# Cache pages on two DMA queues, GEMM pieces one step earlier in long head rows, and gate memsets behind a weight split

## The chip, the cores and the metric

One Trainium2 chip, one of its cores. The metric is the device time of one launch in microseconds (us), lower is better. The engines are named as in the profile: PE (TensorE, matmul), PEld (its weight loads), DVE (VectorE), ACT (ScalarE), POOL (GpSimd) and SP (SyncE, which only issues DMAs).

## What is computed

The reference is one inference step of a two-layer decoder, run for a prompt group (1 x 1024 tokens) and for a sample group (8 sequences x 4 tokens) that share all weights; `D_MODEL` is 1024.

```python
# layer 0: gated width-3 convolution (512 channels) beside differential attention, 4 heads
attn = diff_attend(q, k, v, causal_mask, lam)                    # prompt: own keys
past_k = cache_k[j, page_table].reshape(nb, -1, DA_HEADS, 128)   # samples: 2048 cached keys each
past_v = cache_v[j, page_table].reshape(nb, -1, DA_HEADS, 128)
attn = diff_attend(q, concat(past_k, k), concat(past_v, v), mask, lam)
h = h + rmsnorm(concat([y_conv, attn]) @ w_out0, g[1]);  h = h + rmsnorm(swiglu(rmsnorm(h, g[2])), g[3])
# layer 1: mLSTM, 4 heads of width 256, gates from two more columns per head, chunkwise scan
h = h + rmsnorm(mlstm(rmsnorm(h, g[0]) @ w_in1) @ w_out1, g[1]);  h = h + rmsnorm(swiglu(...), g[3])
```

The cache of the samples is 8 sequences x 16 pages x 128 tokens, for keys and for values, so 256 pages of 128 x 512 float32 (256 KB). Which page is read is known only from `page_table`.

## The kernel before

All 1056 tokens (1024 + 32) lie along the free dimension. A weight matrix is worked through in **visits**: a visit is one panel of 128 output columns (`VISITS`, its weight tile is 512 KB), and has three **units**, each a third of the tokens (352) in one PSUM bank. A weight tile is loaded by SP into one of two buffers (`load_tile`, L200), split by ACT and DVE into a high and a low float16 part (`split_hi`, L218; `split_lo`, L231), and a unit is 24 matmuls (L248). `panel(..., ring=...)` (plan at L270 to L320) says which PSUM banks a visit's units take in turn; a unit waits until the one before it in its bank has been evacuated by ACT or DVE.

Every engine has its instruction stream written out by hand. Where a chain of dependent steps with waits (attention of a head, the sample attention, an mLSTM chunk) runs beside a GEMM, both are Python generators, and `woven(chunk, fill, between)` interleaves them: after each step of the chunk it takes as many steps of the GEMM as the table `between` says. A GEMM step on PE is half a unit, 12 matmuls; the same table is used on PE, ACT, DVE and, for the samples, SP, so a number that moves in it moves work on all of them.

- **Heads of the prompt attention** (`pe_head`, `act_head`, `dve_head`, table `HEAD_FILL`). A head has 8 rows of 128 queries. A row i of 4 or more has three chunk steps on PE: scores of row i+1 and transposes of the first four probability tiles (L843, L846, L908), transposes of the rest (L908), and probabilities times values (L922). The last one waits for the copies of the transposed tiles out of PSUM by ACT (L973) and DVE (L1064). `dve_mixed` (L1002 to L1004) makes the weights of row i+1, and the first transposes of row i+1 wait for them.
- **Sample attention** (`pe_samples`, table `SAMPLE_FILL`). Two rounds of four sequences. In a round come 32 steps on key pages (two pages in a step are transposed, L1155, and multiplied with the queries, L1143), a softmax, and 32 steps on value pages (L1194). Pages go through a ring of 16 buffers. `load_page` reads the page number into a register (L1088), waits until the buffer's last page is used, and issues the DMA (L1092). All pages are issued by SP, in `sp_samples`, woven with the `load_tile` calls of the GEMM beside it. POOL meanwhile waits for the last page (L2061), to restore `hT` from its spill.
- **Start of layer 1** (`act_gates`, `dve_gate_zeros`, `dve_gates`, `dve_mlstm`). POOL spills `hT` to HBM (L2077); gate rows, masks and states then take its place. `dve_gate_zeros` (L1435 to L1440) waits for the spill and clears them. `dve_gates` is the chain of gate computations, taken step by step between the evacuations of the first head's projections (`dve_qkvo`); ACT takes part in it (`act_gate_logs`, L1422, L1424) before it evacuates its first unit (L1509). The projections of one mLSTM head are 8 visits, 24 units, in banks 6 and 7.

Of the kernel before, what the change touches and what calls it, by code (L numbers as in the profile page):

```python
# [72 lines left out]
def build(nc, x_p, x_s, cache_k, cache_v, state_conv, state_C, state_n, state_m, page_table, norms, w_in0,  # L73
# [3 lines left out]
    with ctx:  # L77
# [229 lines left out]
        for i in range(HEADS):  # L307
            for m in range(8):
                c0 = (m // 2) * D + (m % 2) * P + i * MLD
                panel(w_cols(w_in1[0], slice(c0, c0 + P)), KD, "dve" if m in (2, 3) else "act", ring=(6, 7))  # L310
# [504 lines left out]
        HEAD_FILL = (0,) + (1,) * 5 + (1, 0) * 3 + (1, 1) + (1, 0, 1) * 4  # L815
# [269 lines left out]
        def load_page(sp, f):  # L1085

            cache, b, p = (cache_k, cache_v)[f // 64 % 2], 4 * (f // 128) + f // NPG % 4, f % NPG
            page = sp.value_load(page_ids[0:1, b * NPG + p:b * NPG + p + 1], min_val=0,  # L1088
                                 max_val=cache_k.shape[1] - 1)
            if f >= RING:  # L1090
                sp.wait_ge(page_used, f - RING + 1)
            sp.dma_start(ring[:, f % RING, :], cache[0, ds(page, 1), :, :, :].rearrange("a t h e -> (a t) (h e)")  # L1092
                         ).then_inc(page_loaded[f % RING // 2], 16)

        def sp_samples(sp):
            f = RING
            for _ in range(3):
                yield
            for _ in range(2):
                for _ in range(32):  # L1100
                    for f in range(f, min(f + 2, 256)):
                        load_page(sp, f)
                    f += 1
                    yield
                for _ in range(4):
                    yield
                for _ in range(32):
                    for f in range(f, min(f + 2, 256)):
                        load_page(sp, f)
                    f += 1  # L1110
                    yield
                for _ in range(3):
                    yield
# [328 lines left out]
        def dve_gates(dve, chain):  # L1442

            drained(dve, last_unit(GATES))
# [524 lines left out]
        def _(sp):  # L1969
# [28 lines left out]
            for f in range(RING):  # L1998
                load_page(sp, f)
# [14 lines left out]
        def _(pool):  # L2014
# [35 lines left out]
            pool.sem_inc(const_ready, 1)  # L2050

# [8 lines left out]
            pool.dma_start(v_s[0].rearrange("b t h e -> (b t) h e"), kv_s_nat[:, 1, :, :]).then_inc(rows_saved, 16)  # L2060
            pool.wait_ge(page_used, 2 * NB * NPG)  # L2061
# [108 lines left out]
        def _(dve):  # L2170
# [41 lines left out]
            dve_gate_zeros(dve, chain)  # L2212
# [89 lines left out]
```

## Time and profile before

| | |
|---|---|
| median of 3 runs | 3062.14 us (3059.71 to 3066.23) |
| profiled execution | 3063.34 us, of which the span of the trace is 3061.6 us |
| granted TensorE clock, mean | 0.964 |
| PE, PEld, DVE, ACT, POOL busy | 92%, 61%, 34%, 27%, 7% |
| moved by DMA | 225.5 MB, 74 GB/s over the span |

The stages by the trace, in us from the start of the span: prompt heads to about 370, sample attention to 682, output projection and first FFN to about 1588, mLSTM to about 2240, second FFN and output to the end. A busy share of PE near 100% over a whole stage says only that it is not idle; what matters is each place where it is idle, and what ended that.

### The profile page before, as it was taken

The page shows a single profiled execution, that of the slowest core. Times are in us where ns is not written, and L with a number is a line of the kernel's source. Part 1 is how long each engine was busy: PE and PEld are TensorE (multiplying, and loading weights), DVE is VectorE, ACT ScalarE, POOL GpSimd, SP SyncE. Part 2 cuts the span into 40 slices and gives each one's busy share as a digit, 9 for nine tenths or more (in the row PEclk, how much of TensorE's full clock was granted, in tenths as well). Part 3 has the DMA queues.
Part 4 walks back from the last instruction along what each step waited for, and adds up shares of the span by engine and source line. Part 5 has one row for each costly group of instructions (what it writes and reads, how often), then busy time and mean ns, then how long its engine had stood idle before and what let it go on. Part 6 is the DMA issues. An engine that isn't in the chain of part 4 may idle for free.

```text
span 3061.6 us, 46331 instructions
## 1 busy us (share of the span) xinstructions
PE 2831.3 (92%) x19359; PEld 1863.7 (61%) x19359; DVE 1043.0 (34%) x1743; ACT 831.3 (27%) x1523; POOL 210.4 (7%) x189
## 2 busy tenths in 40 slices
PE   6988898979699999999969999999978999999997
PEld 4665554546466666666635767666645666666665
DVE  4454541412622211222263343344454221122223
ACT  4444431313322212221132333333333222122211
POOL 2000000002200000000120010101131000000010
PEclk8999998999799999999989999999989999999998
DMA  5211177771011211112226232422221111111111
GB/s 185 63 56 37 39 217 234 229 250 49 14 49 49 59 45 42 55 50 57 33 63 65 35 87 34 88 47 66 75 78 42 49 51 57 38 50 55 57 40 57
DMA packets 259018, 225.51 MB, mean 74 GB/s; under 512 B 10308, under 2 KB 217466, under 8 KB 258300
## 3 DMA queue, kind: packets, MB, share of 16 engines
q1 hardware_dynamic: 251196, 183.02, 23.3%
q0 software_dynamic: 7616, 39.53, 3.5%
q8 instruction: 155, 2.54, 0.3%
q14 instruction: 51, 0.42, 0.0%
HBM read 195.70 MB, written 26.81 MB: 73 GB/s over the span
## 4 chain that ended last, share of the span: by engine, by line
PE 83%; DVE 6%; SPq 3%; issue 3%; ACT 2%; DMA 2%; POOL 1%; DVEq 0%; ACTq 0%; POOLq 0%; PEldq 0%
PE ps L248 68%; DVE arena L521 2%; PE ps L1155 2%; PE ps L922 1%; SPq L1088 1%; SPq L1092 1%; PE ps L843 1%; PE ps L1716 1%; PE ps L1707 1%; PE ps L1685 1%; POOL arena L334 1%; PE ps L1660 1%; PE ps L1699 1%; PE ps L1143 1%; DVE arena L444 1%
## 5 line engine op out<-in xcount | busy, mean ns | idle before, releaser
L248 PE MATMUL ps<-u,w_split 128*128 128x352 f16 (+1 forms) x10440 | 1625.9, 316 | 67.4 <-DVE u L470 38.7
L248 PEld LDWEIGHTS ps<-u,w_split 128*128 128x128 f16 (+1 forms) x10440 | 1023.5, 99 | 631.5 <-DVE u L470 44.2
L248 PE MATMUL ps<-arena,w_split 128*128 128x352 f16 x4320 | 651.9, 313 | 0.0
L248 PEld LDWEIGHTS ps<-arena,w_split 128*128 128x128 f16 x4320 | 422.1, 98 | 223.9 <-issue 3.2
L231 DVE SCALAR_TENSOR_TENSOR w_split<-w_raw,w_split 128x1024 f16<-128x1024 f32 (+2 forms) x194 | 269.1, 1387 | 835.8 <-ACT w_split L218 835.7
L218 ACT ACTIVATE w_split<-w_raw 128x1024 f16<-128x1024 f32 (+2 forms) x194 | 211.6, 1090 | 84.4 <-PE ps L248 76.2
L577 ACT ACTIVATE arena<-arena 128x352 f16<-128x352 f32 x132 | 65.6, 497 | 390.1 <-DVE arena L609 390.1
L609 DVE SCALAR_TENSOR_TENSOR arena<-ps,arena 128x352 f32<-128x352 f32 x132 | 69.2, 524 | 287.3 <-PE ps L248 287.3
L571 ACT ACTIVATE arena<-ps 128x352 f32<-128x352 f32 x132 | 60.8, 463 | 329.3 <-PE ps L248 329.3
L1509 ACT ACTIVATE arena<-ps 128x352 f32<-128x352 f32 x72 | 33.2, 463 | 207.7 <-PE ps L248 207.6
L331 POOL COPY arena<-arena 128x1056 f32<-128x1056 f32 x4 | 4.3, 1063 | 1227.5 <-ACT arena L590 1203.3
L334 POOL TENSOR_TENSOR arena<-arena 128x1056 f32<-128x1056 f32 x28 | 68.5, 2447 | 236.1 <-ACT arena L590 175.6
L1155 PE MATMUL ps<-ident,hT 128*128 128x128 f32 x512 | 70.4, 281 | 9.0 <-DMA hT<-in_cache_k 7.2
L1155 PEld LDWEIGHTS ps<-ident,hT 128*128 128x128 f32 x512 | 56.2, 142 | 33.1 <-issue 17.7
L585 ACT ACTIVATE arena<-ps 128x352 f32<-128x352 f32 x48 | 22.2, 463 | 193.3 <-PE ps L248 193.3
L626 DVE SCALAR_TENSOR_TENSOR arena<-ps,arena 128x352 f32<-128x352 f32 x48 | 25.0, 521 | 142.3 <-PE ps L248 142.3
L590 ACT ACTIVATE arena<-arena 128x1056 f32<-128x1056 f32 x16 | 17.3, 1083 | 202.2 <-DVE arena L626 202.2
L603 DVE TENSOR_TENSOR arena<-arena 128x352 f16<-128x352 f32 x132 | 68.4, 518 | 8.8 <-ACT arena L577 8.8
L1281 DVE COPY arena<-ps 128x512 f32<-128x512 f32 x64 | 44.2, 691 | 69.4 <-PE ps L1155 69.0
L405 PE MATMUL ps<-arena,ones 128*128 128x352 f32 x144 | 53.4, 530 | 15.3 <-ACT arena L342 15.1
L995 DVE TENSOR_REDUCE small<-ps 128x1 f32<-128x128 f32 (+7 forms) x64 | 45.5, 752 | 60.0 <-PE ps L846 60.0
L1194 PE MATMUL ps<-hT,arena 128*4 128x128 f32 x1024 | 40.1, 291 | 27.2 <-DMA hT<-in_cache_v 27.2
(337 smaller groups left out, 2020.8 us busy)
## 6 DMA issues: line engine op xcount, KB each, us to landing
w_raw<-in_w_gu SPq DMA_DIRECT2D x88, 512.0 KB, 3.8
hT<-in_cache_k SPq DMA_DIRECT2D x128, 256.0 KB, 3.1
hT<-in_cache_v SPq DMA_DIRECT2D x128, 256.0 KB, 3.1
w_raw<-in_w_in SPq DMA_DIRECT2D x56, 512.0 KB, 6.4
w_raw<-in_w_down SPq DMA_DIRECT2D x32, 704.0 KB, 4.6
h_spill<-hT POOLq DMA_DIRECT2D x2, 4224.0 KB, 13.2
hT<-h_spill POOLq DMA_DIRECT2D x2, 4224.0 KB, 13.7
hT<-in_state_C POOLq DMA_DIRECT2D x32, 256.0 KB, 4.2
```

The source lines that it names most:

```text
L218: act.activation(w_split[:, v % 2, 0, 0:kt * n], w_raw[:, v % 2, 0:kt * n], ACT.Copy, scale=WS).then_inc(w_hi, 1)
L231: dve.scalar_tensor_tensor(w_split[:, v % 2, 1, 0:kt * n], w_raw[:, v % 2, 0:kt * n], WS, w_split[:, v % 2, 0, 0:kt * n], ALU.mult, ALU.su ...
L248: ins = pe.matmul(ps[0:m, bank, 0:GW], w_split[:, v % 2, wp, k * w + col * P:k * w + col * P + m], x[:, xp, k0 + k, cols(g)], start=(k == ...
L334: pool.tensor_tensor(ssq, ssq, sq[k % 2], ALU.add).then_inc(ssq_added, 1)
L405: ins = pe.matmul(ps[:, root_bank(n) + g, 0:GW], ones[:, :], sq[k % 2][:, g * GW:(g + 1) * GW], start=(k == 0), stop=(k == KD - 1))
L521: dve.scalar_tensor_tensor(tmp[k % 4], hT[:, k, :], gains[:, col + k:col + k + 1], rs, ALU.mult, ALU.mult).then_inc(t_ready, 1)
L571: act.activation(gate[:, cols(g)], ps[:, UNITS[n].bank, 0:GW], ACT.Silu, scale=1 / WS).then_inc(evac["act"], 1)
L577: act.activation(hid[:, 0, i, cols(g)], hidf[:, cols(g)], ACT.Copy).then_inc(hid_hi, 1)
L603: dve.tensor_tensor(hid[:, 1, i, cols(g)], hidf[:, cols(g)], hid[:, 0, i, cols(g)], ALU.subtract).then_inc(hid_ready, 1)
L609: dve.scalar_tensor_tensor(hidf[:, cols(g)], ps[:, UNITS[n].bank, 0:GW], 1 / WS, gate[:, cols(g)], ALU.mult, ALU.mult).then_inc(evac["dve" ...
L995: dve.tensor_reduce(neg_mx[:, n % 4:n % 4 + 1], score_cols(i, c)[:, 0:(i + 1) * P], AX.X, ALU.max, negate=True).then_inc(nm_ready, 1)
L1155: ins = pe.transpose(ps[:, 4 + e, h * P:(h + 1) * P], ring[:, f % RING, h * P:(h + 1) * P], ident[:, :])
```

## The change

1. **Pages on two queues.** Pages f with f // 2 odd (2, 3, 6, 7, ...) are issued by POOL, the others by SP. POOL issues its 8 pages of the first 16 after it has built `smask`, and the other 120 after it has stored the keys and values of the prompt and the new rows of the samples, in one loop, ahead of its wait for the last page. SP keeps its steps; in every second one it issues nothing.
2. **`HEAD_FILL`** in rows 4 to 7: the table for a row is (1, 1, 0) in place of (1, 0, 1), so the second GEMM piece of the row runs ahead of the product with the values instead of after it.
3. **Gate memsets.** `dve_gate_zeros` moves from ahead of `dve_mlstm` into the first step of `dve_gates`, behind the split of the second projection tile. The projections of the first mLSTM head use banks 1 to 7 in turn instead of 6 and 7.

```diff
-                panel(w_cols(w_in1[0], slice(c0, c0 + P)), KD, "dve" if m in (2, 3) else "act", ring=(6, 7))
+                panel(w_cols(w_in1[0], slice(c0, c0 + P)), KD, "dve" if m in (2, 3) else "act",
+                      ring=(6, 7) if i else (1, 2, 3, 4, 5, 6, 7))
...
-        HEAD_FILL = (0,) + (1,) * 5 + (1, 0) * 3 + (1, 1) + (1, 0, 1) * 4
+        HEAD_FILL = (0,) + (1,) * 5 + (1, 0) * 3 + (1, 1) + (1, 1, 0) * 4
...
                 for _ in range(32):
-                    for f in range(f, min(f + 2, 256)):
+                    if f // 2 % 2 == 0 and f < 2 * NB * NPG:
                         load_page(sp, f)
-                    f += 1
+                        load_page(sp, f + 1)
+                    f += 2
                     yield
...
         def dve_gates(dve, chain):
 
+            dve_gate_zeros(dve, chain)
+            yield
             drained(dve, last_unit(GATES))
...
             for f in range(RING):
-                load_page(sp, f)
+                if f // 2 % 2 == 0:
+                    load_page(sp, f)
...
             pool.sem_inc(const_ready, 1)
+            pool.wait_ge(ids_loaded, 16)
+            pool.wait_ge(x_spilled, 16)
+            pool.wait_ge(t_ready, KD)
+            for f in range(RING):
+                if f // 2 % 2:
+                    load_page(pool, f)
...
             pool.dma_start(v_s[0].rearrange("b t h e -> (b t) h e"), kv_s_nat[:, 1, :, :]).then_inc(rows_saved, 16)
+            for f in range(RING, 2 * NB * NPG):
+                if f // 2 % 2:
+                    load_page(pool, f)
             pool.wait_ge(page_used, 2 * NB * NPG)
...
             split_lo(dve, QKVO)
-            dve_gate_zeros(dve, chain)
             dve_mlstm(dve, chain)
```

How the instructions stand in the two programs, at the three places of which the prediction speaks. (Line numbers of the changed program run a little ahead: L1093 is L1092 before, L923 is L922, L1438 is L1435.)

POOL, behind the last stores of the prompt heads. Before:

```order
L2059 DMA out<-kv_s_nat 32x512 [waits k_ev,v_ev]
L2060 DMA out<-kv_s_nat 32x512
L2062 DMA hT<-h_spill 128x8448 [waits page_used]
L2064 DMA out<-arena 2x512 [waits conv_ev]
L2065 DMA out<-arena 16x512
```

POOL at the same place in the changed program:

```order
L2071 DMA out<-kv_s_nat 32x512 [waits k_ev,v_ev]
L2072 DMA out<-kv_s_nat 32x512
L1089 TENSOR_LOAD page_ids
L1089 ISA x2
L1093 ISA [waits page_used]
L1093 DMA hT<-in_cache_k 128x512
```

The last four rows repeat 120 times (for keys and values), and SP has as many of them fewer. The eight earlier ones stand ahead of the stores of the heads.

PE, row 5 of a head. Before:

```order
L908 MATMUL ps<-ident,arena 128x128 [waits pt_ev_act,w_comb]
L908 MATMUL ps<-ident,arena 128x128
L922 MATMUL ps<-arena 128x128 [waits v_ev,pv_ev,pt_ev_dve,pt_ev_act]
L922 MATMUL ps<-arena 128x128 x5
L248 MATMUL ps<-u,w_split 128x352 x12
L843 MATMUL ps<-arena 128x512 [waits p_ready]
```

PE in the changed program, the same row 5:

```order
L909 MATMUL ps<-ident,arena 128x128 [waits pt_ev_act,w_comb]
L909 MATMUL ps<-ident,arena 128x128
L248 MATMUL ps<-u,w_split 128x352 x12
L923 MATMUL ps<-arena 128x128 [waits v_ev,pv_ev,pt_ev_dve,pt_ev_act]
L923 MATMUL ps<-arena 128x128 x5
L844 MATMUL ps<-arena 128x512 [waits p_ready]
```

The piece of 12 GEMM matmuls now stands between the transposes and the product that waits for their copies; the scores of the next row follow the product directly.

DVE at the start of layer 1, before:

```order
L231 SCALAR_TENSOR_TENSOR w_split<-w_raw,w_split 128x1024 [waits w_hi]
L1435 MEMSET hT 4x1056 [waits spilled]
L1436 MEMSET hT 4x8 [waits dve_c]
L1437 MEMSET hT 4x8
L1438 MEMSET m_prev 4x1
L1439 MEMSET acol 128x108
L1440 MEMSET hT 128x576
L231 SCALAR_TENSOR_TENSOR w_split<-w_raw,w_split 128x1024 [waits w_hi]
L1445 SCALAR_TENSOR_TENSOR arena<-arena 4x1056 [waits evac_act]
```

DVE at the start of layer 1 in the changed program:

```order
L231 SCALAR_TENSOR_TENSOR w_split<-w_raw,w_split 128x1024 [waits w_hi] x2
L1438 MEMSET hT 4x1056 [waits spilled]
L1439 MEMSET hT 4x8 [waits dve_c]
L1440 MEMSET hT 4x8
L1441 MEMSET m_prev 4x1
L1442 MEMSET acol 128x108
L1443 MEMSET hT 128x576
L1450 SCALAR_TENSOR_TENSOR arena<-arena 4x1056 [waits evac_act]
```

The second split now stands ahead of the wait for the spill; the gate chain still stands behind it.

## Rows read from the trace of the kernel before

**Rows 1.** The page: chain that ended last, shares of the span by line.

```profile
PE ps L248 68%; DVE arena L521 2%; PE ps L1155 2%; PE ps L922 1%; SPq L1088 1%; SPq L1092 1%; PE ps L843 1%; PE ps L1716 1%; PE ps L1707 1%; PE ps L1685 1%; POOL arena L334 1%; PE ps L1660 1%; PE ps L1699 1%; PE ps L1143 1%; DVE arena L444 1%
```

**Rows 2.** Windows: length, PE, PEld, DVE, ACT, POOL busy (instructions), clock, DMA share, GB/s.

```profile
64.00:81.00 17.00, 17.00 (x116) 11.01 (x115) 2.27 (x3) 2.03 (x4) 0.55 (x2) 1.00 0.81 240
622.00:667.00 45.00, 30.15 (x440) 16.54 (x432) 7.77 (x15) 1.55 (x2) 0.00 (x0) 0.89 0.81 246
```

**Rows 3.** Timeline of SP's queue: start, length of the series, line, what, how many.

```profile
63.62 17.68 SPq L1092 DMA_DIRECT2D hT<-in_cache_k  x16
...
445.22 1.06 SPq L200 DMA_DIRECT2D w_raw<-in_w_in  x2
452.60 34.89 SPq L1092 DMA_DIRECT2D hT<-in_cache_v  x26
```

**Rows 4.** The page: DMA issues, count, KB each, median us from issue to landing.

```profile
hT<-in_cache_v SPq DMA_DIRECT2D x128, 256.0 KB, 3.1
...
hT<-in_state_C POOLq DMA_DIRECT2D x32, 256.0 KB, 4.2
```

**Rows 5.** Timeline of PE, sample attention: start, us, [idle before <- what ended it].

```profile
452.00 0.62 PE L1194 MATMUL ps<-hT,arena 128*4 128x128 f32 x16
457.32 3.68 PE L248 MATMUL ps<-u,w_split 128*128 128x352 f16 x12 [4.71 <-DVE arena L807]
...
517.89 0.62 PE L1194 MATMUL ps<-hT,arena 128*4 128x128 f32 x16
528.64 1.04 PE L1155 MATMUL ps<-ident,hT 128*128 128x128 f32 x8
...
591.21 0.90 PE L1166 MATMUL ps<-arena 128*32 128x32 f32 x32
611.22 0.62 PE L1194 MATMUL ps<-hT,arena 128*4 128x128 f32 x16
617.13 1.49 PE L1194 MATMUL ps<-hT,arena 128*4 128x128 f32 x48
671.02 0.62 PE L1194 MATMUL ps<-hT,arena 128*4 128x128 f32 x16
```

**Rows 6.** Chain in order of time, first key pass: start, us, what.

```profile
387.53 1.90 PE ps L248 x12
...
402.02 1.90 PE ps L248 x12
```

**Rows 7.** Timeline of POOL: DMAs it issues.

```profile
293.24 0.90 POOL L2055 DMA_DIRECT2D out<-arena  x1 [2.63 <-DVE arena L1041]
...
1673.80 2.92 POOL L2091 DMA_DIRECT2D hT<-in_state_C  x4 [27.91 <-ACT hT L1431]
```

**Rows 8.** Waits of PE in the prompt heads (us in total, times, longest).

```profile
PE ps L922 <- issue: 22.5, 16, 4.5
```

**Rows 9.** Timeline of PE and DVE, heads 1 and 3.

```profile
195.28 1.96 PE L922 MATMUL ps<-arena 128*128 128x128 f32 x12 [3.39 <-issue]
197.03 3.28 PE L248 MATMUL ps<-u,w_split 128*128 128x352 f16 x12
218.89 1.09 PE L870 MATMUL ps<-ident,arena 128*128 128x128 f32 x8 [0.80 <-ACT arena L725]
337.81 2.90 PE L922 MATMUL ps<-arena 128*128 128x128 f32 x12 [4.54 <-issue]
339.13 1.28 DVE L756 SCALAR_TENSOR_TENSOR arena<-arena,gains 128x1024 f32<-128x1024 f32 x1
```

**Rows 10.** Timeline of all engines at the start of layer 1.

```profile
1594.57 10.13 PE L248 MATMUL ps<-u,w_split 128*36 128x352 f16 x66 [0.77 <-DVE u L470]
1599.90 1.04 ACT L218 ACTIVATE w_split<-w_raw 128x1024 f16<-128x1024 f32 x1
1605.04 0.94 DVE L1435 MEMSET hT<- 4x1056 f32 x1 [8.15 <-DMA h_spill<-hT]
1613.23 32.06 PE L248 MATMUL ps<-u,w_split 128*128 128x352 f16 x204 [8.54 <-ACT arena L1509]
```

More of the change, by code:

```diff
@@ L1083, in build, with load_page @@
         SAMPLE_FILL = (1, 1, 0) + ROUND_FILL * 2
-        def load_page(sp, f):
+        def load_page(eng, f):
             cache, b, p = (cache_k, cache_v)[f // 64 % 2], 4 * (f // 128) + f // NPG % 4, f % NPG
-            page = sp.value_load(page_ids[0:1, b * NPG + p:b * NPG + p + 1], min_val=0,
+            page = eng.value_load(page_ids[0:1, b * NPG + p:b * NPG + p + 1], min_val=0,
                                  max_val=cache_k.shape[1] - 1)
             if f >= RING:
-                sp.wait_ge(page_used, f - RING + 1)
-            sp.dma_start(ring[:, f % RING, :], cache[0, ds(page, 1), :, :, :].rearrange("a t h e -> (a t) (h e)")
+                eng.wait_ge(page_used, f - RING + 1)
+            eng.dma_start(ring[:, f % RING, :], cache[0, ds(page, 1), :, :, :].rearrange("a t h e -> (a t) (h e)")
                          ).then_inc(page_loaded[f % RING // 2], 16)
@@ L1107, in sp_samples @@
                 for _ in range(32):
-                    for f in range(f, min(f + 2, 256)):
+                    if f // 2 % 2 == 0 and f < 2 * NB * NPG:
                         load_page(sp, f)
-                    f += 1
+                        load_page(sp, f + 1)
+                    f += 2
                     yield
```

## The prediction

> **What bounds the kernel now.** I start with the chain that ended last [rows 1]. The GEMM matmuls of PE make 68% of it, and nothing in this change makes them faster or fewer. The two rows to look at are SPq L1088 and L1092: they are SP's page issue, the only queue among the large entries, and with the waits of PE behind them they are what part 1 aims at. I then look for PE's idle places one stage at a time, since over the whole span PE is 92% busy.
>
> In the sample attention SP issues 16 pages in 17.68 us, 1.105 us each, at a time when it waits for nothing [rows 3]. A page is 256 KB, so this is 240 GB/s, and the windows show just that, with the DMA engines busy 0.81 of the time [rows 2]. In the second pass over values (622 to 667) the rate is the same, 246 GB/s at 0.81, while PE is busy 30 of 45 us. So the page stream runs at the pace of SP's issue, and the DMA engines have a fifth of their time left. PE waits, and its clock falls to 0.89 there.
>
> In the prompt heads PE waits 22.5 us in all, 16 times, ahead of L922 [rows 8]: rows 4 to 7 of four heads. At the start of layer 1 it waits 8.54 us for ACT [rows 10], which waits for DVE, which waits for the spill of `hT`.
>
> **The cost of each part.**
>
> *Pages, value passes.* First the time of a page once SP is not the limit. 240 GB/s at 0.81 and 246 GB/s at 0.81 [rows 2] are 296 and 304 GB/s at a full share; 256 KB at 300 is 0.87 us. I take that. Below it no page gets faster than PE uses it. Above it the bound is the 1.05 to 1.1 us of today, if 0.81 is already all that these 2 KB rows allow.
>
> A value pass has 64 pages, of which 16 wait in the ring. From its first step to its last PE needs 48 more: 48 x 0.87 = 41.8, plus two weight tiles of 512 KB in the same engines (2 x 1.75), plus 3.1 to land [rows 4] and 0.6 for the first step, together 49.0 us. PE alone needs less: three steps take 1.49 [rows 5] and the GEMM piece behind them 1.9 [rows 6], so 32 steps take 10.7 x 3.4 = 36, some 38 with the small products. Measured from first to last step are 452.00 to 517.89, 65.9 us, and 611.22 to 671.02, 59.8 us [rows 5]. The gain is 16.9 + 10.8 = 27.7 us.
>
> The first of these also holds a stall of 4.71 us at 457.32 for DVE. Its cause is in SP's stream: the weight tile is issued at 445.22 [rows 3], behind 16 value pages. With half of these pages gone from SP it is issued 8 x 1.1 = 8.8 us sooner, and the stall is covered. It lies inside the 65.9, so I don't count it again.
>
> *Pages, key passes.* PE needs 14.49 us for 8 steps and a GEMM piece (387.53 to 402.02, [rows 6]), 0.91 us a page, so at 0.87 pages are never late. From the second step to the end of the pass that is 3 x 14.49 + 7 x 1.59 + 1 = 55.6 us, where 528.64 to 591.21 are 62.6 [rows 5]: a gain of 7.0. The first pass catches up with SP only in its last steps; I count nothing. Sum of part 1: 34.7 us.
>
> *POOL's price.* No row shows a page, or any register load, issued on POOL. From the nearest rows: a 256 KB DMA costs it 2.92 / 4 = 0.73 us, and a store of 1024 short rows 0.90 [rows 7]. SP's whole period of 1.1 added to the dearer of these gives 2.0 us a page at most, 0.73 at least. I take 1.5, since SP's period already holds its own DMA instruction. POOL has every second page, so what counts is half of it, 0.75, against 0.87. POOL's DMAs land in 4.2 us where SP's take 3.1 [rows 4]; a ring of 16 hides 1.1 us. Queued behind the new waits on POOL stand the restore of `hT` and the stores of `conv_nat`, which waited for the last page before too, so they lose nothing. The stores of the heads stand behind POOL's first 8 pages only, and those are issued some 10 us before them.
>
> *A rule against it.* The share of 0.81 speaks for free DMA time. The Trainium skill says (DMA: Bandwidth & Descriptors, "Issuing engines are not separate DMA queues") that DMAs from all engines run on the same 16 DMA engines, and that issuing from several saves only the sequencers' time. By that rule the gain is SP's issue time, which the rows show to be the limit here; if it were not, the rival below would hold.
>
> *`HEAD_FILL`.* The wait ahead of L922 is for copies of transposed tiles. A GEMM piece of 1.9 us now stands in it. Four long waits, one in row 5 of each head (3.39 in head 1, 4.54 in head 3, [rows 9]), shrink by 1.9 each: 7.6. The long ones sum to some 14.7, so the other twelve make 7.8 us, each under 1.9 and covered whole. Behind a long wait PE runs at a lower clock, so that a GEMM piece takes 3.28 [rows 9] instead of 1.90, 1.4 us in each head: 5.6. Sum 21.0. Given back: behind row 7 the piece covered the evacuation of the product, and PE now waits about 0.9 at L870 where it waited 0.80, so nothing. In head 3 DVE takes the two convolution taps, 1.28 each [rows 9], ahead of the weights of the next row: 1 us, my estimate. I take 20. If the clock still falls it is 14, and if DVE's later evacuations hold the transposes of rows 5 and 6 it is 8; at most it is the 22.5 and some clock, 26.
>
> *Gates.* PE stops at 1594.57 + 10.13 = 1604.7, since banks 6 and 7 are full and ACT cannot evacuate before the gate logs, and goes on at 1613.23 [rows 10]. With seven banks it takes the third unit at once. The next tile is split by ACT at 1599.90 to 1600.94 and by DVE now at about 1602, not behind the spill (1605.04 and the memsets). Two visits are 6 units of 3.58, of which 4 are left at 1604.7: 14.3 us, until 1619. By then ACT is free (1612.6), has evacuated three units and split the tile after that, and DVE its part at about 1619. So the 8.5 us go, less up to 0.5 for this next split: 8 us. Wider banks alone don't help elsewhere.
>
> Sum: 34.7 + 20 + 8 = 62.7 us. The profiled execution took 3063.3 us, so it would take 3000.6; the median of the runs is 1.2 lower, and I predict **3000**.
>
> **The rivals.**
>
> *The DMA engines are the limit already.* For it: with 2 KB rows the share never passes 0.82 while only pages run, and the rate never 250 GB/s. Against it: SP's steady period, which needs no full DMA engine. A page then stays at 1.05 us and a value pass takes 0.6 + 50.4 + 3.5 + 3.1 = 57.6 us: gains of 8.3 and 2.2, none in the key passes. Part 1 brings 10, all together 38: 3024 us.
>
> *Pages are faster than I say*, since 0.81 overstates what a page occupies. Then PE limits the value passes, 39 us each: 27 + 21 + 7 = 55, the sum 83: 2979 us.
>
> *POOL is the new bound, and the kernel gets slower.* Place: the TENSOR_LOAD of the page number and the descriptors on POOL. Pages come in order, so its period P gives P / 2 a page on every pass. At P = 2.18 that is today's pace. At P = 3 each pass needs 0.6 + 48 x 1.5 + 3.1 = 75.7 us: 9.8 and 15.9 more in the value passes, 13 and some 18 in the key passes, 57 in all, less 28 from the other parts: 3091 us. Each 0.1 us of P is 4 x 48 x 0.05 = 9.6, so it decides from P = 2.7. Against it stand the 0.73 and 0.90 of [rows 7]. If DVE's work held POOL up, P would grow by DVE's busy share, 7.77 of 45 us in the value pass [rows 2], from 1.5 to 1.8, still not late. The Trainium skill (SBUF — State Buffer, "SBUF: two separate sides") says that while DVE runs a two-port operation GpSimd can't write descriptors, which is this rival's mechanism; no row before shows it on a page.
>
> *The moved pieces bring nothing*, since the waits behind L922 only move to the next transposes: 12 us less than forecast, 3012; inside the range.
>
> **How the numbers follow.** The forecast has 0.62, the DMA limit 0.16, faster pages 0.12, POOL 0.08, of which 0.06 above P = 2.7; 0.02 are left for something that cancels out near zero. A measurement of this kernel tells 0.2%, 6 us, from no change: faster 0.92, same 0.02, slower 0.06. The forecast's own range is 2984 to 3014 (0.85 or 0.95 us a page, with the bounds of part 2). The range takes in both the DMA limit at 3024, with a weaker part 2 (3036), and faster pages, not quite with everything else at its best: 2974 to 3036.
>
> **What would show it.** In the changed profile: pages of SP and POOL alternate, the period of one page over both queues is near 0.87, the DMA share in the value passes is above 0.9 at 290 GB/s or more; first to last value step takes 49 us twice, the second key pass 56; the stage of the samples ends some 55 us earlier, 20 of these from the heads. PE's waits at L922 (then L923) are four of about 1.5 to 2.6 us. At the start of layer 1 PE has no wait for ACT, and at most 0.5 us for the third projection tile. I am wrong if the DMA share stays at 0.81 or rises without more GB/s, if POOL's DMAs are more than 2.2 us apart with pages free, or if PE waits at the first transposes of rows 5 to 7.

## The result, and the profile after

| | before | changed |
|---|---|---|
| median | 3062.76 us of 4 runs (3059.71 to 3066.23) | 2992.11 us of 4 runs (2990.08 to 2995.70) |
| span of the profiled execution | 3061.6 us | 2988.7 us |
| granted TensorE clock, mean | 0.964 | 0.973 |
| PE busy | 92% | 94% |

The changed kernel is faster by 70.7 us: ratio 0.977, 95% interval 0.9753 to 0.9787. The spans differ by 72.9 us. The forecast was 62.7 us less and 3000, the range 2974 to 3036.

**The chain that ended last**, by line, from the page of the changed kernel [rows 1]:

```profile
PE ps L248 71%; PE ps L1158 2%; DVE arena L522 2%; PE ps L1146 1%; PE ps L844 1%; PE ps L1721 1%; PE ps L1712 1%; PE ps L923 1%; PE ps L1690 1%; POOL arena L335 1%; DMA hT<-in_cache_v 1%; PE ps L1665 1%; PE ps L1704 1%; PE ps L1197 1%; DVE arena L445 1%
```

SP's page issue (SPq L1088 and L1092 before) is gone from the large entries, and a transfer, `hT<-in_cache_v`, stands among them. The GEMM matmuls have a larger share of a shorter span.

**Windows** in the two value passes of the changed kernel [rows 2]; the columns are length, busy time of PE, PEld, DVE, ACT and POOL with instructions, clock, DMA share, GB/s:

```profile
440.00:490.00 50.00, 43.17 (x609) 27.19 (x600) 9.85 (x22) 10.20 (x23) 15.95 (x30) 1.00 0.97 344
572.00:620.00 48.00, 38.22 (x535) 23.72 (x534) 13.68 (x31) 6.81 (x17) 10.60 (x20) 0.96 0.93 335
```

The rate rose from 246 to 335 and 344 GB/s, and the clock from 0.89 to 0.96 and 1.00. Both windows run on past the last value step (472.94 and 606.14, below), so they mix stretches in which the engines are full with others in which they are not. Shorter windows of the same trace, the first at the start of a pass, the others in its middle:

```profile
430.00:435.00 5.00, 5.00 (x72) 3.25 (x70) 0.53 (x1) 0.26 (x1) 1.07 (x2) 1.00 0.37 109
445.00:470.00 25.00, 19.18 (x336) 11.73 (x338) 0.07 (x1) 1.20 (x3) 9.16 (x18) 1.00 1.05 382
572.00:592.00 20.00, 14.17 (x235) 8.83 (x237) 1.05 (x2) 0.00 (x0) 5.82 (x11) 0.91 1.04 378
```

In the middle of a pass the DMA engines are full and move 378 to 382 GB/s, which is 0.69 us for a page of 256 KB. At its start they are not: 109 GB/s.

**Timeline of PE** in the sample attention [rows 5]: start, us, what, and the idle time before it with what ended that.

```profile
426.83 0.62 PE L1197 MATMUL ps<-hT,arena 128*4 128x128 f32 x16
429.88 1.95 PE L248 MATMUL ps<-u,w_split 128*128 128x352 f16 x12 [2.43 <-DVE arena L808]
...
472.94 0.62 PE L1197 MATMUL ps<-hT,arena 128*4 128x128 f32 x16
...
540.05 0.90 PE L1169 MATMUL ps<-arena 128*32 128x32 f32 x32
...
560.06 0.62 PE L1197 MATMUL ps<-hT,arena 128*4 128x128 f32 x16
...
606.14 0.62 PE L1197 MATMUL ps<-hT,arena 128*4 128x128 f32 x16 [0.60 <-DMA hT<-in_cache_v]
```

From first to last step a value pass takes 46.1 us, twice, where it took 65.9 and 59.8. The stall of 4.71 us at the start of the first is 2.43.

**One line's instructions**, the page issue (duration in ns, min/median/max), with PE's waits for it and the time to landing:

```profile
L1093 SPq DMA_DIRECT2D hT<-in_cache_v x64: 337/338/5187, 391.9 to 596.0; - x64
...
L1093 POOL DMA_DIRECT2D hT<-in_cache_v x64: 536/536/545, 395.7 to 598.9; - x64
...
who waited for it (us, times):
  PE ps L1197: 11.6, 9
...
DMA to landing us min/median/max: 2.5/4.5/12.5
```

POOL's price is steady: 0.54 us for the DMA. SP's is usually 0.34, but one took 5.19 us. A page, of keys or values, lands in a median of 4.5 us over both queues where it took 3.1, and in 12.5 at most. PE still waits 11.6 us for value pages (27.2 before), and no longer for key pages.

**Timeline of POOL** in the first value pass [rows 7]:

```profile
443.35 0.54 POOL L1093 DMA_DIRECT2D hT<-in_cache_v  x1 [0.63 <-PE ps L1197]
444.51 0.54 POOL L1093 DMA_DIRECT2D hT<-in_cache_v  x1 [0.63 <-issue]
```

POOL's period is 1.165 us, a price that no row of before showed. The 0.63 us ahead of the DMA are the register load and its arithmetic.

**Waits of PE** in the prompt heads [rows 8], and **the timeline** of PE and DVE in row 5 of one head [rows 9]:

```profile
PE ps L923 <- issue: 7.5, 4, 2.7
```

```profile
184.99 1.95 PE L248 MATMUL ps<-u,w_split 128*128 128x352 f16 x12
188.54 1.58 PE L923 MATMUL ps<-arena 128*128 128x128 f32 x12 [1.60 <-issue]
```

```profile
186.88 1.22 DVE L231 SCALAR_TENSOR_TENSOR w_split<-w_raw,w_split 128x1024 f16<-128x1024 f32 x1 [2.11 <-ACT w_split L218]
188.02 0.42 DVE L1065 COPY arena<-ps 128x256 f32<-128x256 f32 x1
```

Sixteen waits of 22.5 us are four of 7.5. What is left in this row ends with DVE's copy, which stands behind a split of weights that itself waits for ACT.

**Timeline** of PE and DVE at the start of layer 1 [rows 10]:

```profile
1529.74 70.54 PE L248 MATMUL ps<-u,w_split 128*36 128x352 f16 x471 [0.77 <-DVE u L471]
```

```profile
1536.14 1.23 DVE L231 SCALAR_TENSOR_TENSOR w_split<-w_raw,w_split 128x1024 f16<-128x1024 f32 x1 [4.09 <-ACT w_split L218]
1540.41 0.94 DVE L1438 MEMSET hT<- 4x1056 f32 x1 [3.04 <-DMA h_spill<-hT]
1552.57 1.23 DVE L231 SCALAR_TENSOR_TENSOR w_split<-w_raw,w_split 128x1024 f16<-128x1024 f32 x1
```

PE runs through, where it stood 8.54 us. The split at 1552.57, the third tile's, is never waited for.

Where the 72.9 us are, by the stages of both traces: 22.1 ahead of the first key step (370.45 to 348.32), 42.7 in the samples (first key step to the first L248 of the output projection, 311.0 to 268.3 us), none up to the layer 1 spill (910.7 in both), 8.1 behind it.

### The profile page after: what moved, and what is told of

It is laid out like the page before. It is cut to its first block, busy times and chain, and to the rows that moved or that the text cites. A ratio compares the mean times of both kernels' runs of the same rounds, so it can differ in the third digit from the quotient of the medians.

```text
span 2988.7 us, 46335 instructions
## 1 busy us (share of the span) xinstructions
PE 2803.8 (94%) x19359; PEld 1857.4 (62%) x19359; DVE 1042.8 (35%) x1743; ACT 831.8 (28%) x1523; POOL 279.3 (9%) x317
## 4 chain that ended last, share of the span: by engine, by line
PE 87%; DVE 6%; ACT 2%; issue 1%; POOL 1%; DMA 1%; SPq 1%; DVEq 0%; ACTq 0%; POOLq 0%; PEldq 0%
PE ps L248 71%; PE ps L1158 2%; DVE arena L522 2%; PE ps L1146 1%; PE ps L844 1%; PE ps L1721 1%; PE ps L1712 1%; PE ps L923 1%; PE ps L1690 1%; POOL arena L335 1%; DMA hT<-in_cache_v 1%; PE ps L1665 1%; PE ps L1704 1%; PE ps L1197 1%; DVE arena L445 1%
## 5 line engine op out<-in xcount | busy, mean ns | idle before, releaser
L248 PE MATMUL ps<-u,w_split 128*128 128x352 f16 (+1 forms) x10440 | 1608.1, 314 | 55.7 <-DVE u L471 37.8
L248 PEld LDWEIGHTS ps<-u,w_split 128*128 128x128 f16 (+1 forms) x10440 | 1017.5, 98 | 608.5 <-DVE u L471 43.4
L248 PE MATMUL ps<-arena,w_split 128*128 128x352 f16 x4320 | 651.9, 313 | 0.0
L248 PEld LDWEIGHTS ps<-arena,w_split 128*128 128x128 f16 x4320 | 422.2, 98 | 223.8 <-issue 3.2
L332 POOL COPY arena<-arena 128x1056 f32<-128x1056 f32 x4 | 4.3, 1064 | 1227.5 <-ACT arena L591 1203.3
L1284 DVE COPY arena<-ps 128x512 f32<-128x512 f32 x64 | 44.2, 691 | 60.2 <-PE ps L1158 59.7
L996 DVE TENSOR_REDUCE small<-ps 128x1 f32<-128x128 f32 (+7 forms) x64 | 45.5, 752 | 41.3 <-PE ps L847 41.3
L1227 ACT ACTIVATE arena<-ps 128x512 f32<-128x512 f32 x64 | 38.3, 598 | 72.1 <-PE ps L1158 72.1
```

Of the source, the lines that this page charges most:

```text
L248: ins = pe.matmul(ps[0:m, bank, 0:GW], w_split[:, v % 2, wp, k * w + col * P:k * w + col * P + m], x[:, xp, k0 + k, cols(g)], start=(k == ...
L996: dve.tensor_reduce(neg_mx[:, n % 4:n % 4 + 1], score_cols(i, c)[:, 0:(i + 1) * P], AX.X, ALU.max, negate=True).then_inc(nm_ready, 1)
```

## The experiments

The table reads three places in every trace: the start of the first key step, the stage of the samples from there to POOL's first copy of the norm behind it (L331, L332 in the changed kernel), and the two value passes, from first to last value step. A ratio is against runs of the kernel before on the same chip; the medians come from several chips, on which that kernel took 3061.2 to 3063.1 us.

| kernel | median | ratio, 95% interval | first key step | samples | value passes |
|---|---|---|---|---|---|
| before | 3062.8 | | 370.5 | 323.7 | 65.9, 59.8 |
| changed | 2992.1 | 0.9770 (0.9753 to 0.9787) | 348.3 | 281.0 | 46.1, 46.1 |
| e1_pages | 3025.8 | 0.9883 (0.9868 to 0.9898) | 368.7 | 283.9 | 46.4, 47.2 |
| e2_headfill | 3038.6 | 0.9928 (0.9914 to 0.9942) | 348.5 | 318.7 | 61.3, 57.5 |
| e3_gates | 3051.9 | 0.9972 (0.9962 to 0.9982) | 366.5 | 323.9 | 66.3, 59.0 |
| e4_ring_only | 3056.1 | 0.9983 (0.9974 to 0.9992) | 366.8 | 326.6 | 66.9, 60.2 |
| s1_sp_const | 3017.7 | 0.9855 (0.9839 to 0.9872) | 368.9 | 277.6 | 45.0, 42.3 |
| s2_pool_2loads | 3034.3 | 0.9907 (0.9891 to 0.9924) | 348.7 | 326.5 | 64.0, 61.0 |
| s3_pool_3loads | 3091.6 | 1.0093 (1.0076 to 1.0110) | 349.0 | 386.5 | 75.4, 72.1 |
| s4_all_pool | 3044.7 | 0.9943 (0.9926 to 0.9959) | 348.3 | 336.4 | 67.6, 63.2 |
| x3_five_eighths | 2994.3 | 0.9774 (0.9760 to 0.9787) | 346.6 | 284.7 | 48.9, 45.5 |
| x1_fills | 2979.1 | 0.9725 (0.9712 to 0.9739) | 338.1 | 284.6 | 47.1, 48.3 |
| x4_head_only | 2983.9 | 0.9750 (0.9736 to 0.9763) | 340.7 | 283.0 | 47.0, 47.3 |
| x5_head_fill3 | 2992.3 | 0.9774 (0.9761 to 0.9787) | 340.4 | 295.5 | 47.5, 48.2 |

How far one trace may be read: where nothing of a stage was changed, it scatters by some 3 us (323.7, 323.9 and 326.6 in the samples), the first key step by 4 (370.5 to 366.5), and what lies behind the samples by another 4 (2367.4 us before, 2371.0 and 2371.1 in `e1_pages` and `e2_headfill`, which have the same program there).

### Each part alone

Pages on two queues alone, `e1_pages`:

```diff
-                panel(w_cols(w_in1[0], slice(c0, c0 + P)), KD, "dve" if m in (2, 3) else "act",
-                      ring=(6, 7) if i else (1, 2, 3, 4, 5, 6, 7))
+                panel(w_cols(w_in1[0], slice(c0, c0 + P)), KD, "dve" if m in (2, 3) else "act", ring=(6, 7))
...
-        HEAD_FILL = (0,) + (1,) * 5 + (1, 0) * 3 + (1, 1) + (1, 1, 0) * 4
+        HEAD_FILL = (0,) + (1,) * 5 + (1, 0) * 3 + (1, 1) + (1, 0, 1) * 4
...
```

The diff is against the changed kernel; the memsets are back in their place as well.

> Only the page issue is split between SyncE and GpSimd; head filler and gate part as before. If the three parts add up as the two traces suggest (the sample stage from 311.0 to 268.3 us), this run is 42.7 us faster than before, 3020 us, with first to last value step at 46 us in both passes. Rival: a part of these 42.7 us comes from the head filler (a higher clock on entry, earlier weight tiles); then this run brings 35 us or less and the value passes take 49 us or more.

`HEAD_FILL` alone, put into the kernel before:

```diff
-        HEAD_FILL = (0,) + (1,) * 5 + (1, 0) * 3 + (1, 1) + (1, 0, 1) * 4
+        HEAD_FILL = (0,) + (1,) * 5 + (1, 0) * 3 + (1, 1) + (1, 1, 0) * 4
```

> Only HEAD_FILL is changed. If the parts add up: 22 us faster, 3041 us, all of it ahead of the first key step (about 348 us instead of 370), and the sample stage keeps its 311 us, because SyncE's page issue sets its pace. Rival: the page stream does not follow the earlier start (its own transfers were already late), and the stage gives some of it back: 10 to 15 us in all.

Ring and memsets alone, put into the kernel before:

```diff
+                      ring=(6, 7) if i else (1, 2, 3, 4, 5, 6, 7))
...
+            dve_gate_zeros(dve, chain)
+            yield
             drained(dve, last_unit(GATES))
...
-            dve_gate_zeros(dve, chain)
             dve_mlstm(dve, chain)
```

> Only the bank ring of the first head and the place of the gate memsets are changed. Theory: 8 us faster, 3054.5 us, and PE has no wait for ACT at the start of layer 1. Rival: the wait comes back at a later tile of the same head and this brings under 3 us.

Measured against the 3061.2 us of the kernel before on that chip: pages 35.4 us (31 to 40 by the interval), `HEAD_FILL` 22.7 (18 to 26), gates 9.4 (6 to 12), together 67.5. The three parts add up to the 70.7 of the whole within what the intervals allow, so no large part of the gain needs two of them together. The theory of `e1_pages` had 42.7 us, and that lies outside the 31 to 40 measured. Its rival isn't borne out either: the median is near that rival's 35, but the value passes are at 46.4 and 47.2, not 49. By the trace the sample stage is 39.8 us shorter, which the scatter of 3 us doesn't set apart from 42.7; the 3.6 us that its trace loses behind the samples are within the scatter there. In `e2_headfill` nothing is given back in the samples: the stage is 318.7 us, 5 under before, and the first value pass 61.3. Whether `HEAD_FILL` helps a little there or this is scatter, one trace can't tell.

The wide ring alone:

```diff
-                panel(w_cols(w_in1[0], slice(c0, c0 + P)), KD, "dve" if m in (2, 3) else "act", ring=(6, 7))
+                panel(w_cols(w_in1[0], slice(c0, c0 + P)), KD, "dve" if m in (2, 3) else "act",
+                      ring=(6, 7) if i else (1, 2, 3, 4, 5, 6, 7))
```

> Only the bank ring of the first head is widened to seven banks; the memsets stay ahead of the split. Theory (the banks were the cause; with six units in hand PE needs the third tile only about 14 us after it would have stopped, and DVE comes out of the memsets long before): as fast as the run with both halves, 7 to 8 us under before. Rival (both halves are needed): PE now stops for the third tile's split behind the spill and the memsets, 3 us or more, and only 3 to 5 us are gained.

It brought 5.1 us (2 to 8). Timeline of PE and of DVE there:

```profile
1593.70 24.45 PE L248 MATMUL ps<-u,w_split 128*36 128x352 f16 x162 [0.77 <-DVE u L471]
1619.44 64.61 PE L248 MATMUL ps<-u,w_split 128*128 128x352 f16 x432 [1.29 <-DVE w_split L231]
```

```profile
1604.17 0.94 DVE L1436 MEMSET hT<- 4x1056 f32 x1 [8.15 <-DMA h_spill<-hT]
...
1605.91 1.15 DVE L231 SCALAR_TENSOR_TENSOR w_split<-w_raw,w_split 128x1024 f16<-128x1024 f32 x1
...
1618.15 1.23 DVE L231 SCALAR_TENSOR_TENSOR w_split<-w_raw,w_split 128x1024 f16<-128x1024 f32 x1
```

The wait for banks is gone by the ring alone. The interval of 2 to 8 us doesn't tell the theory's 7 to 8 from the rival's 3 to 5, so the trace has to. What comes in its place is neither of the two expectations: not the second tile's split behind the memsets (1605.91, early enough) but the third's (1618.15), because the second split stands behind the memsets here, inside the gate chain, and pushes what follows back: from the first memset to the third split it takes 13.98 us. In `e3_gates` it takes 12.16 (1600.46 to 1612.62), and PE has no wait. From one norm to the next the mLSTM stage takes 809.7 us before, 803.1 with the ring, 800.0 with both: the ring is worth some 7, the memsets some 3, of which only 1.29 are seen as a wait.

### What limits a page

Is it the issue on one queue? `s1_sp_const` keeps all pages on SP and takes the look-up away:

```diff
-            page = sp.value_load(page_ids[0:1, b * NPG + p:b * NPG + p + 1], min_val=0,
-                                 max_val=cache_k.shape[1] - 1)
+            page = b * NPG + p
```

> The kernel before, all pages on SyncE, but each page's number is a constant in the program instead of read from the page table (so the outputs of the sample heads come from other pages than the table's). Left out: the register load, its arithmetic and its bounds test, some 0.7 of the 1.105 us that SyncE spends on a page. Theory (the issue time of one queue was the limit, nothing else about it): as fast as the run with the pages alone on two queues, 3026 us (3020 to 3032), value steps at 46 us. Rival 1 (one queue can't carry more than about 250 GB/s): no gain, 3055 us or more. Rival 2 (part of the gain comes from GpSimd's kind of queue being easier on the DMA engines): between, 3035 to 3045 us, with a DMA share over 0.9 but under 320 GB/s.

Against 3062.8 us it brought 45.1 us. Timeline of SP's queue and windows of that run:

```profile
62.56 8.67 SPq L1091 DMA_DIRECT2D hT<-in_cache_k  x16
...
449.41 18.61 SPq L1091 DMA_DIRECT2D hT<-in_cache_v  x26
```

```profile
460.00:480.00 20.00, 17.08 (x309) 10.44 (x308) 2.19 (x3) 1.91 (x3) 0.00 (x0) 1.00 1.04 370
595.00:615.00 20.00, 17.75 (x286) 10.84 (x279) 3.13 (x8) 1.06 (x1) 0.00 (x0) 0.91 1.06 382
```

SP issues a page in 0.54 us where the engines have room, 0.56 less than before (the expectation had 0.7 less), and in 18.61 / 26 = 0.72 where they fill up. So one queue is enough, the limit before was the 1.105 us of look-up and issue, and both rivals fall. The Trainium skill (DMA: Bandwidth & Descriptors, "Issuing engines are not separate DMA queues") says that DMAs from all issuing engines run on the same 16 DMA engines, and that issuing from several only saves the time of issue. By that rule the trace agrees: one queue moves 370 and 382 GB/s once its issue is cheap, two queues moved 378 and 382. The median is below the theory's range, 3020 to 3032, and 8 us under `e1_pages`, most of it in the second value pass (42.3 against 47.2). That is not explained: the rate with full engines is the same in both, but the pages of this run also lie in order in memory, which the table's do not, and it uses no GpSimd queue.

How dear may POOL's issue be? More register loads ahead of each of POOL's pages, two or three of them:

```diff
+            for _ in range(2 if f // 2 % 2 else 0):
+                eng.value_load(page_ids[0:1, f % NPG:f % NPG + 1], min_val=0, max_val=cache_k.shape[1] - 1)
             page = eng.value_load(page_ids[0:1, b * NPG + p:b * NPG + p + 1], min_val=0,
```

> The changed kernel with two more register loads (results unused) ahead of every page on GpSimd. A load with what follows it costs 1.165 - 0.54 - 0.07 = 0.56 us, so GpSimd's period P becomes 2.29 us. Theory (P / 2 sets the page once it is above 0.76 us in the value passes and 0.88 us in the key passes): value passes 0.6 + 48 x 1.145 + 3.1 = 58.7 us instead of 46.1, key passes 3 us longer: 28 to 31 us over the changed kernel, 3022 us. Rival (the ring of 16 and SyncE's share hide a late GpSimd): under 10 us lost, below 3002.

> As the run before, with three more loads: P = 2.85 us. Theory: value passes 0.6 + 48 x 1.425 + 3.1 = 72 us, 26 us over the changed kernel in each, key passes about 72 instead of 56, 16 us each: 83 us lost, 3075 us, just above the kernel before, with which the point where GpSimd makes the kernel slower lies between this run and the one with two loads. Rival as there: under 20 us lost.

Timeline of POOL in the first of these and in the second:

```profile
472.94 0.54 POOL L1095 DMA_DIRECT2D hT<-in_cache_v  x1 [1.70 <-issue]
```

```profile
470.17 0.54 POOL L1095 DMA_DIRECT2D hT<-in_cache_v  x1 [2.24 <-issue]
```

The periods are 2.24 and 2.78 us. The losses against the changed kernel are 42 and 99 us, more than the 30 and 83 expected, and far from hidden. The value passes are near the sum (64.0 and 61.0 for 58.7; 75.4 and 72.1 for 72). The key passes are not: the second takes 64.8 and 81.2 us. The gap between the first value pass and the second key pass is 8 to 9 us, in which a POOL with a period of 2.8 issues three of its eight pages; the sum had let every pass start with a full ring. That this makes the loss in the key passes is argued from these numbers; no run isolates it. Between the two runs the time rises 57.3 us for 0.54 us of period, so the kernel before would be met at 2.24 + 28.5 / 106 = 2.5 us. The real 1.165 us is far below that.

All pages on POOL, SP keeps the weights:

```diff
             for f in range(RING):
-                if f // 2 % 2:
-                    load_page(pool, f)
+                load_page(pool, f)
```

> The changed kernel, but all pages are issued by GpSimd and none by SyncE; weight tiles stay on SyncE. Theory (the issue period of the one queue is the limit): 1.165 us a page, value passes 0.6 + 48 x 1.165 + 3.1 = 59.6 us, key passes 60 instead of 56: 30 to 38 us over the changed kernel, 3022 to 3030 us; DMA share near 0.75, 225 GB/s. It would still be faster than the kernel before less its other two parts (3029 us), since no weight tile stands in the page queue. Rival (GpSimd's queue moves pages faster than its issue suggests, or the gain is from leaving SyncE): within 10 us of the changed kernel.

Windows of that run in its value passes:

```profile
440.00:500.00 60.00, 42.48 (x604) 23.29 (x592) 4.55 (x7) 4.27 (x7) 26.46 (x50) 0.86 0.77 227
610.00:660.00 50.00, 32.72 (x441) 17.54 (x439) 7.77 (x15) 1.55 (x2) 21.06 (x39) 0.84 0.78 233
```

256 KB in 1.165 us are 225 GB/s, and 227 and 233 were moved: again the period of one queue is the rate. At 52 us over the changed kernel it lost more than the 30 to 38 expected. It is also 14 us above what the kernel before would take with the other two parts (3062.8 - 22.7 - 9.4 = 3030.7), where the expectation had it a little under: all pages on POOL were worse than all pages on SP. The second key pass takes 67.0 us, and the first value pass stops early: with a full ring no page is issued while PE stands in the stall at the pass's start.

Does the share of the two queues matter?

```diff
-                    if f // 2 % 2 == 0 and f < 2 * NB * NPG:
+                    if f // 2 % 8 not in (1, 4, 7) and f < 2 * NB * NPG:
```

> The changed kernel with five of eight page pairs on SyncE and three on GpSimd (slots 1, 4 and 7 of the ring) instead of four and four. SyncE's share then sets 1.105 x 5/8 = 0.69 us a page, a little under the 0.76 that the engines gave with both queues and at the 0.69 (375 GB/s) that they gave when SyncE issued constant pages alone. Theory (pages by GpSimd's queue take more of the DMA engines): value passes 43.5 to 45 us instead of 46.1, 2 to 5 us gained, 2987 to 2990. Rival (one of two equal queues blocks at 0.76 whatever the shares): within 1 us of the changed kernel. Second rival (SyncE, with its weight tiles and held up by full engines for up to 5 us at a time, is late again): 3 us or more lost.

2994.3 us, 2 us over the changed kernel and inside the intervals: no gain. The theory, that pages by GpSimd's queue take more of the DMA engines, has no support from it. Its 0.76 us with both queues came from the long windows; with full engines both queues together were at 0.69 already.

### A better version

```diff
-        HEAD_FILL = (0,) + (1,) * 5 + (1, 0) * 3 + (1, 1) + (1, 1, 0) * 4
+        HEAD_FILL = (0,) + (1,) * 5 + (1, 0) * 4 + (1, 1, 0) + (1, 1, 1) + (1, 1, 0) * 2
...
-        ROUND_FILL = ((1, 0, 0, 0, 0, 0, 0, 0) * 4 + (2, 2, 2, 2) + (1, 0, 0) * 10 + (1, 0) + (1, 1, 1))
+        ROUND_FILL = ((1,) + (0,) * 15) * 2 + (2, 2, 2, 2) + (1, 0, 1, 0, 0) * 6 + (1, 0) + (1, 1, 1)
```

> The changed kernel with GEMM pieces placed anew in two stages, which are read apart in the trace. Samples: two of the four pieces of each key pass go to the value pass behind it (13 pieces there instead of 11), where PE waits 11.6 us for pages. Theory: each key pass is 2 x 1.9 = 3.8 us shorter, the value passes stay at 46 to 47.5 us (the third weight tile in them costs 1.5 us of DMA time): 4 to 7 us gained in this stage. Rival: the pieces crowd DVE's evacuation of their single bank, or pages follow the earlier start with nothing in hand, and the value passes grow by 4 us or more: nothing gained. Heads: the second piece of row 3 goes behind the products' place in row 5, ahead of the wait that is left at L923 (7.5 us in 4 times). Theory: these four go and row 3 gets none over 0.9 us, 4 to 7 us gained ahead of the first key step (now 348.3). Rival: row 3 gets a wait of 1.5 us or more in each head, and it comes out even. Both theories: 2980 to 2984 us; both rivals: 2992.

The first of these edits alone, then that edit with one moved piece in the samples instead of two:

> The changed kernel with only the head part of the version before: the second piece of row 3 now ahead of row 6, behind row 5's product. In the run with both parts this stage ended 10.2 us earlier (338.1 instead of 348.3), while the stage of the samples was 3.6 us longer (284.6 instead of 281.0). Theory (the 13 pieces of the value pass brought nothing: a wait for DVE and a lower clock between key and value pass took back what the key passes gave): 8 to 11 us under the changed kernel, 2981 to 2984 us by the medians, and 0 to 4 us faster than the version with both parts by the stage times (profiled span 2976 to 2980). Rival (the longer stage was chance): as fast as or slower than the version with both parts, span 2980 or more.

```diff
+        ROUND_FILL = ((1, 0, 0, 0, 0, 0, 0, 0) * 2 + (0,) * 8 + (1,) + (0,) * 7 + (2, 2, 2, 2) + (1, 0, 0) * 8
+                      + (1, 0) * 4 + (1, 1, 1))
```

> As the run before, but one of four pieces (the third, not the last) goes from each key pass to its value pass: pieces at steps 0, 8 and 24, twelve in the value pass. Theory (two moved pieces were harmful because of the place ahead of the softmax, and PE has 5.8 us of waiting in each value pass that one piece fits into): key passes 1.9 us shorter each, the stretch between the passes 20.4 us as in the changed kernel, value passes up to 0.5 us longer: 2 to 4 us under the run before. Rival (the value passes are bound by the DMA engines, which get the weight tile as well, 1.5 us of their time): the pass grows by as much, within 1 us of the run before.

*Heads.* The first key step starts 7.6 to 10.2 us earlier in all three, where `x1_fills` had expected 4 to 7, and the waits at L923 fall from 7.5 us to 0.4. Timeline of PE and DVE in row 5 of the same head, `x4_head_only`:

```profile
181.27 1.95 PE L248 MATMUL ps<-u,w_split 128*128 128x352 f16 x12
183.06 1.50 PE L923 MATMUL ps<-arena 128*128 128x128 f32 x12
184.40 1.95 PE L248 MATMUL ps<-u,w_split 128*128 128x352 f16 x12
```

```profile
181.70 0.41 DVE L1065 COPY arena<-ps 128x256 f32<-128x256 f32 x1
183.17 1.23 DVE L231 SCALAR_TENSOR_TENSOR w_split<-w_raw,w_split 128x1024 f16<-128x1024 f32 x1 [1.06 <-ACT w_split L218]
```

The moved piece stands behind the product of row 5, so it can't cover the wait in row 5, as the expectation of `x1_fills` had it. What it does is to bring the end of a weight tile one step later: DVE now copies ahead of the split, not behind it.

*Samples.* Moving pieces from the key passes brought nothing that shows (stage 284.6 us with it, 283.0 without), and one piece fewer did harm: 8.3 us over `x4_head_only`, where the theory had 2 to 4 under and the rival no change. By the medians the version with both edits is 4.8 us under the one with the heads alone, by the stages it is not, and the span of `x4_head_only`, 2980.7, is on the side of its rival; that stays open. Timeline of PE between key and value pass of `x5_head_fill3`, and of DVE there:

```profile
537.85 1.96 PE L248 MATMUL ps<-u,w_split 128*128 128x352 f16 x12
541.88 3.74 PE L248 MATMUL ps<-u,w_split 128*128 128x352 f16 x24 [2.07 <-DVE arena L808]
548.51 3.36 PE L248 MATMUL ps<-u,w_split 128*128 128x352 f16 x12 [2.89 <-DVE arena L808]
```

```profile
538.26 1.27 DVE L757 SCALAR_TENSOR_TENSOR arena<-arena,gains 128x1024 f32<-128x1024 f32 x1
...
539.73 1.28 DVE L760 SCALAR_TENSOR_TENSOR arena<-arena,gains 128x1024 f32<-128x1024 f32 x1
...
541.21 0.52 DVE L808 SCALAR_TENSOR_TENSOR arena<-ps,arena 128x352 f32<-128x352 f32 x1
546.66 0.16 DVE L1296 TENSOR_REDUCE small<-small 128x1 f32<-128x5 f32 x1 [4.93 <-ACT arena L1236]
```

With one piece fewer ahead of it, another piece of the tile falls into the softmax: its two taps hold up the evacuation of the single bank, then the evacuation waits behind the softmax's sums. The stage is 12.5 us longer, 6.2 and 7.5 of it in the two stretches between key and value pass, and all of the gain of the heads is gone. The fastest version by the medians is `x1_fills`: 2979.1 us, 13 us under the changed kernel (their intervals, 0.9712 to 0.9739 and 0.9753 to 0.9787, don't touch).

## Why the prediction was right, and where it was off

**Pages.** The mechanism is shown: SP's issue was the limit, and a second queue or a cheap issue removes it. The term was 34.7 us and measured 35.4 alone (interval 31 to 40), 42.7 in the trace of the whole. Its parts: value passes 16.9 and 10.8 forecast, 19.8 and 13.7 measured; second key pass 7.0 forecast, 6.2 measured; first key pass nothing forecast, 3.6 measured (59.3 to 55.7 us from first to last step, and 57.2 in `e1_pages`, so a part of it may be scatter).

**The page time of 0.87 us** is the step that was off. It came from dividing the rate by the busy share, 246 / 0.81. With full engines a page takes 0.69 us, 378 and 382 GB/s at 1.04 and 1.05, and 370 at 1.04 in `s1_sp_const`; the same division there gives 356 to 364, so the share at a trickle overstates what a page occupies, as one of the rivals said. The trace of before had a sign of it, five microseconds in which a weight tile issued at 627.16 was among the pages:

```profile
630.00:635.00 5.00, 2.04 (x40) 0.91 (x40) 0.00 (x0) 0.00 (x0) 0.00 (x0) 0.82 0.94 318
```

That is more than the 300 GB/s of the forecast, and it also speaks against the rival of full DMA engines, which had said that the rate never passes 250.

Yet the other rival's time, 2979, didn't come: it had PE as the next bound, with value passes of 39 us. They take 46.1, and PE still waits 11.6 us for pages. The forecast's own sum with 0.69 gives 0.6 + 48 x 0.69 + 2 weight tiles at 1.4 + 5.2 to land = 41.7 us, 4.4 too few. What is missing is the start of a pass: the ring is full, a page is issued only when a buffer comes free, and POOL's first page follows 6.0 and 3.7 us behind the first value step, so the engines run below their rate (109 GB/s from 430 to 435) before they are full. How the 4.4 us divide between this and the late landings no run shows. So the pass time of 49 us came near the measured 46.1 in part by luck: the page was forecast too dear, and the slow start was left out.

**The stall of 4.71 us** was said to be covered once its tile is issued sooner. That was half of it. Timeline of DVE at this place in the changed kernel:

```profile
424.03 1.22 DVE L231 SCALAR_TENSOR_TENSOR w_split<-w_raw,w_split 128x1024 f16<-128x1024 f32 x1
...
426.24 1.28 DVE L757 SCALAR_TENSOR_TENSOR arena<-arena,gains 128x1024 f32<-128x1024 f32 x1
...
427.73 1.28 DVE L760 SCALAR_TENSOR_TENSOR arena<-arena,gains 128x1024 f32<-128x1024 f32 x1
...
429.21 0.52 DVE L808 SCALAR_TENSOR_TENSOR arena<-ps,arena 128x352 f32<-128x352 f32 x1
```

The split no longer waits for a tile, but the taps still stand ahead of the evacuation for which PE waits, and 2.43 us of it stay. It lay inside the value pass, so it changed no term of the forecast.

**POOL's price** was taken at 1.5 us from 0.73 to 2.0, and is 1.165. It is half of that per page that counts, 0.58, under 0.69, so the size didn't matter. The rival in which POOL makes the kernel slower was sound in kind: at 2.78 us it does. Its point was put at 2.7 and lies at about 2.5 by the two runs; that a slow POOL also can't refill the ring between the passes is the likely reason. POOL's 64 value pages took 536 to 545 ns each, with DVE busy 9.85 of 50 us from 440 to 490: nothing held its descriptors up. The Trainium skill (SBUF — State Buffer, "SBUF: two separate sides") has it that some DVE operations do this; no run here shows it.

**`HEAD_FILL`**: 20 forecast, 22.7 measured (18 to 26). The four waits left and their size (1.5 to 2.6 forecast, 1.60 to 2.7 measured) are as forecast. So is that L870 gives nothing back, 0.72 for 0.80. The taps' 1 us in head 3 is 1.9 at L909, in two waits, ahead of the first transposes of rows 6 and 7. A wait there was one of the prediction's signs of being wrong: it came, but small, and the three other heads have none.

**Gates**: 8 forecast, 9.4 measured (6 to 12). That the banks are the cause and the third tile's split isn't waited for is shown. That the memsets were only a detail is not quite so: 3 of these us are theirs.

**The sum** against the spans, 62.7 for 72.9, is short by 10.2 us: 8.0 in the samples (34.7 for 42.7), 2.1 ahead of them (20 for 22.1), 0.1 in the gates. The kernel before has its first key step the latest of the five traces with the same heads (366.5 to 370.5), so a part of the 2.1 is scatter. The 8.0 are 2.9 in each value pass and 3.6 in the first key pass, less 0.8 in the second and 0.6 between the first key and the first value pass.

## What to carry to other kernels

When a queue issues at an even period while nothing waits for it, compute the rate from that period: it is the limit, whatever the busy share of the DMA engines says, and the share at that rate doesn't tell the ceiling. Read the ceiling from a stretch in which the engines are full throughout: a window that also holds the start or the end of a pass gave 344 GB/s where the engines move 382. Splitting the issue over a second, idle queue works as long as its own period, divided by its part, stays under the page time; count the start of each pass too, and what must be refilled between passes. Where fill work is placed by a table, look at which evacuation and which weight split each moved piece brings along: a piece in one place gained 8 us and one in another lost 12.

## What was not expected of the hardware

- The DMA engines moved 227 GB/s at a share of 0.77 and 240 at 0.81, but 370 at 1.04 and 382 at 1.05. The rate rises faster than the share.
- With the engines full, an issue on SP's queue can be held: 5.19 us at most in the changed kernel (median 0.34 for value pages), 4.14 on a key page and 3.66 on a value page in `s1_sp_const` (medians 0.37 and 0.43). POOL's issues in the changed kernel took 0.59 us at most.
- With full engines one queue and two moved the same, 370 to 382 GB/s, and a share of five to three instead of four to four between the queues changed nothing that can be told.
- A register load with its arithmetic, on POOL, costs 0.54 us (from 1.165 to 2.24 us for two), as much as the DMA instruction behind it.
